# Expert choice of tiles 1 to 3 moved one unit sooner, and the order of the row gathers with it

## The reference

```python
q = (t @ wq).reshape(PEER_BLOCK, PEER_HEADS, 2, PEER_DQ // 2)
s = jnp.einsum('tpcd,pckd->tpck', q, sub_keys)
s1, i1 = lax.top_k(s[:, :, 0], PEER_TOPK)
s2, i2 = lax.top_k(s[:, :, 1], PEER_TOPK)
cand = s1[..., :, None] + s2[..., None, :]        # 16 x 16 sums
cidx = i1[..., :, None] * PEER_NKEYS + i2[..., None, :]
top, pos = lax.top_k(cand, PEER_TOPK)             # (flattened)
idx = jnp.take_along_axis(cidx, pos, axis=-1)
g = jax.nn.softmax(top, axis=-1)
a = jax.nn.gelu(jnp.einsum('tpkd,td->tpk', u[idx], t))
return jnp.einsum('tpk,tpkd->td', g * a, v[idx])
```

## Time and profile before

| | |
|---|---|
| median of 3 runs | 3128.29 us (3120.03 to 3139.96) |
| the profiled execution | 3147.13 us, span 3145.3 us |
| busy share of PE, DVE, ACT, POOL | 77%, 61%, 31%, 37% |
| gathers begin and end | 622.3 us, 2438 us |
| first memset of `half(0)` | 1559.13 us |
| mean granted clock of TensorE | 0.871 |

### The profile page before, as it was taken

The page is one execution under the profiler, slowest core; times in us unless marked ns, Lnnn a source line. Parts: engine busy times, 40 slices in busy tenths (PEclk is TensorE's granted clock), DMA queues, the critical chain, the costliest instruction groups (busy, mean ns, idle before and its releaser), DMA issues.

```text
span 3145.3 us, 43836 instructions
## 1 busy us (share of the span) xinstructions
PE 2415.9 (77%) x16608; PEld 1758.0 (56%) x16608; DVE 1930.2 (61%) x4058; ACT 976.8 (31%) x1694; POOL 1154.5 (37%) x1028
## 2 busy tenths in 40 slices
PE   7898996896044545565475898976999999999998
PEld 5666775545000000111174777742677889996998
DVE  3221866488945655476688877764344576666665
ACT  4443655311000000000032433422433455455544
POOL 0000000067755657577756565567455000000000
PEclk8998998998567887788786999976999999998999
DMA  6232111289978989899988999999899545552454
GB/s 270 98 111 83 48 42 53 95 315 352 330 289 316 369 320 360 314 350 348 360 307 304 330 408 408 408 375 336 300 406 397 180 137 179 186 192 68 146 184 147
DMA packets 218945, 803.92 MB, mean 256 GB/s; under 512 B 24432, under 2 KB 27760, under 8 KB 214768
## 3 DMA queue, kind: packets, MB, share of 16 engines
q0 software_dynamic: 147456, 536.94, 45.4%
q1 hardware_dynamic: 71280, 264.19, 23.7%
HBM read 798.93 MB, written 2.10 MB: 255 GB/s over the span
## 4 chain that ended last, share of the span: by engine, by line
PE 33%; DVE 19%; issue 11%; POOL 8%; DMA 7%; another core or an unknown queue 3%; ACT 1%; DVEq 0%; SPq 0%; POOLq 0%; ACTq 0%
PE ps L1817 9%; PE ps L1819 8%; PE ps L1818 8%; DVE pe_ring L2522 7%; PE ps L1757 4%; DMA pe_ring<-in_v,pe_vidx 3%; POOL pe_ring L1700 3%; POOL pe_ring L1706 3%; DVE la_w_lo L2570 3%; DMA pe_ring<-in_u,pe_idx 1%; PE ps L1896 1%; POOL pe_more L1700 1%; PE ps L1905 1%; PE ps L1922 1%
## 5 line engine op out<-in xcount | busy, mean ns | idle before, releaser
L1757 PE MATMUL ps<-pe_ring,pe_spot 128*32 128x512 f32 x1632 | 430.4, 754 | 245.6 <-DMA pe_ring<-in_v,pe_vidx 192.2
L1700 POOL DMA_INDIRECT pe_ring<-in_u,pe_idx x415 | 489.7, 1180 | 289.8 <-issue 178.6
L2522 DVE CUSTOM_DVE_ANT_0 pe_ring<-pe_ring,pe_htok 128x1024 f32<-128x1024 f32 x415 | 495.4, 1222 | 136.8 <-DMA pe_ring<-in_u,pe_idx 119.7
L1817 PE MATMUL ps<-la_h_hi,la_w_hi 128*128 128x256 f32 x1856 | 537.5, 290 | 32.8 <-DVE la_w_lo L2570 21.5
L1819 PE MATMUL ps<-la_h_hi,la_w_lo 128*128 128x256 f32 x1856 | 529.0, 285 | 2.6 <-issue 2.2
L1818 PE MATMUL ps<-la_h_lo,la_w_hi 128*128 128x256 f32 x1856 | 528.2, 285 | 1.8 <-issue 1.7
L1706 POOL DMA_INDIRECT pe_ring<-in_v,pe_vidx x408 | 438.4, 1074 | 236.3 <-issue 115.8
L2570 DVE TENSOR_TENSOR la_w_lo<-la_w_raw,la_w_hi 128x1024 fp32r<-128x1024 f32 (+1 forms) x368 | 440.1, 1196 | 69.3 <-ACT la_w_hi L2182 48.7
L2182 ACT ACTIVATE la_w_hi<-la_w_raw 128x1024 fp32r<-128x1024 f32 (+1 forms) x368 | 379.7, 1034 | 306.6 <-DMA la_w_raw<-in_down 77.8
L1817 PEld LDWEIGHTS ps<-la_h_hi,la_w_hi 128*128 128x128 f32 x1856 | 354.8, 191 | 70.7 <-DVE la_w_lo L2570 33.3
L1757 PEld LDWEIGHTS ps<-pe_ring,pe_spot 128*32 128x32 f32 x1632 | 85.2, 126 | 486.2 <-issue 313.1
(11 more groups left out here) (366 smaller groups left out, 3960.9 us busy)
## 6 DMA issues: line engine op xcount, KB each, us to landing
la_w_raw<-in_gate SPq DMA_DIRECT2D x88, 512.0 KB
la_w_raw<-in_up SPq DMA_DIRECT2D x88, 512.0 KB
la_w_raw<-in_down SPq DMA_DIRECT2D x64, 448.0 KB
la_w_raw<-in_a_in SPq DMA_DIRECT2D x40, 512.0 KB
wring<-in_w_in SPq DMA_DIRECT2D x32, 512.0 KB, 3.8
la_w_raw<-in_down SPq DMA_DIRECT2D x32, 512.0 KB
xT<-in_w_mod SPq DMA_DIRECT2D x8, 1024.0 KB, 4.8
hT<-in_w_mod SPq DMA_DIRECT2D x8, 1024.0 KB, 4.9
```

The source lines that it names most:

```text
L1700: pool.indirect_dma_start(row(n), None, io["u"], bass.IndirectOffsetOnAxis(idx[:, t, j:j + 1], 0)).then_inc(land[GATHERS[n][0]], 16)
L1757: return pe.matmul(ps[PER * grp:PER * grp + PER, half, :], spot[:, j // TOKENS % 2, grp, lo:lo + PER], row(n)[:, half * 512:(half + 1) * 5 ...
L1817: pe.matmul(slot(n), parts_hi[:, n % SPLIT, i, :], hi[:, k, :], start=first, stop=False)
L2522: dve.tensor_tensor_reduce(row(n), row(n), htok[:, t, :], 1.0, 0.0, ALU.mult, ALU.add, dots[:, t % 2, j:j + 1]).then_inc(dot_done, 1)
```

## The change

Three things are changed. In `gathers()` the v rows that stood behind the last unit of tile 1 and behind the last group of tile 2 are put ahead instead: 28 v rows of tile 0 go first in place of 16, and 12 of tile 1 in place of 2. On DVE each choose of tiles 1 to 3 is made one unit sooner (in the groups of tile 2, one group sooner): choose(1,0) and choose(1,1) stand together behind `weigh(0)`, choose(1,2), (1,3) and (2,0) behind dots 31, 63 and 95 of tile 1, choose(2,1) behind `weigh(1)`, and choose(2,2) to (3,3) behind groups 0 to 5 of tile 2; nothing is chosen behind group 6. On ACT the exps follow. `turn_indices(1)` now stands behind v row 96 instead of 108, and `token_indices(1)` behind dot 98 instead of 116.

```diff
-    TURN_AT, SUM_AT, SQUARES_AT = (108, 84), (16, 32), 60
+    TURN_AT, SUM_AT, SQUARES_AT = (96, 84), (16, 32), 60
...
-        v_next = P - 4 * (UNIT_U // 2 + 12)
+        v_next = P - 4 * UNIT_U // 2 - 3 * 12
...
-            if j % UNIT_U == UNIT_U - 1:
+            if j % UNIT_U == UNIT_U - 1 and j + 1 < P:
...
-        v_next = P - GROUPS_U * (GROUP_U + GROUP_V)
+        v_next = P - GROUPS_U * GROUP_U - (GROUPS_U - 1) * GROUP_V
...
-            if j % GROUP_U == GROUP_U - 1:
+            if j % GROUP_U == GROUP_U - 1 and j + 1 < EARLY:
...
             choose(1, 0)
+            choose(1, 1)
             for j in range(HK):
                 dot(1, j)
                 if j % UNIT_U == UNIT_U - 1 and j + 1 < HK:
-                    choose(1, (j + 1) // UNIT_U)
-                if j == 116:
+                    ahead = (j + 1) // UNIT_U + 1
+                    choose(1 + ahead // 4, ahead % 4)
+                if j == 98:
                     token_indices(1)
             weigh(1)
-            choose(2, 0)
+            choose(2, 1)
...
-                choose(2 + (group >= 3), (group + 1) % 4)
+                if group + 1 < GROUPS_U:
+                    choose(2 + (group >= 2), (group + 2) % 4)
```

More of the change, by code:

```diff
@@ L2407, in _ @@
             exps(1, 0)
+            exps(1, 1)
             place_weights(0, 2)
             place_weights(0, 3)
-            exps(1, 1)
+            exps(1, 2)
             place_weights(0, 4)
-            exps(1, 2)
             place_weights(0, 5)
+            exps(1, 3)
             place_weights(0, 6)
-            exps(1, 3)
+            exps(2, 0)
             place_weights(0, 7)
             gelu(1)
-            exps(2, 0)
             place_weights(1, 0)
@@ L2422, in _ @@
             exps(2, 1)
+            exps(2, 2)
             place_weights(1, 2)
-            exps(2, 2)
             place_weights(1, 3)
@@ L2427, in _ @@
             place_weights(1, 4)
+            exps(3, 0)
             square(0)
-            exps(3, 0)
             place_weights(1, 5)
+            exps(3, 1)
             place_weights(1, 6)
-            exps(3, 1)
+            exps(3, 2)
             place_weights(1, 7)
-            exps(3, 2)
             exps(3, 3)
```

## The result

| | before | after |
|---|---|---|
| median of 20 runs each | 3135.39 us (3119.84 to 3162.19) | 3107.03 us (3088.57 to 3124.26) |
| ratio | | 0.9903, 95% interval 0.9880 to 0.9927 |
| the profiled execution | 3147.13 us, span 3145.3 | 3104.64 us, span 3102.8 |
| first memset of `half(0)` | 1559.13 us | 1512.35 us |

The change gains 28 us by the medians (23 to 38 by the interval of the ratio), against 64 forecast: 3107 lies above the range of 3044 to 3098. The prediction's 3128.29 was the median of three runs; over 20 it is 3135.39. The half begins 46.8 us sooner, where 66 were forecast (1493).

A forecast was written before the change was run, and what follows sets the result against it. The prediction took no engine as full all the time, but the stream of gathers, broken by POOL's waits, as the bound. Terms of 14.9 + 30.4 + 15.05 + 4 = 64 us off 3128.3 gave 3064 us, range 3044 to 3098.

The forecast's parts named there:

- Term 1: Start of tile 1: twelve more v rows fill 14.9 us of POOL's 21.31 us wait before u row 0.
- Term 2: Inside tile 1: with chooses a unit sooner, POOL's waits before u rows 32, 64 and 96 go, 30.4 us.
- DVE stays the faster one and catches up: Inside tile 1, a unit of 60 gathers: the stream needs 77 us, DVE's 32 dots and one choose 54 to 71.
- Term 3: Start of tile 2: POOL's 15.05 us wait before u row 0 goes; ACT's two added waits cost 0.
- Term 4: Way into the first half of the last layers: choose(3,3) comes a group sooner; 3.5 to 8.5 us, taken as 4.
- Does the gain last: From gather 568 to the end: the order is the old one, and all 64 us are carried through.
- five waits: POOL's idle before u rows 0, 32, 64, 96 of tile 1 and 0 of tile 2, 66.73 us in sum.
- slower, by the idle without releaser: Rival: POOL's twelve waits without releaser, 870 to 1560 us, each grow to 10.38 us; 31 us slower, 3159; chance 0.05.
- The wait changes its name: Rival: in tile 2 POOL waits for buffers behind late dots; 35 us back, gain 29, 3099 us; chance 0.11.

The follow-up runs named there:

- old_again: The kernel before the change, unaltered, profiled on the same chip as `changed_again`; 3119.3 us in one run, that chip's median of the old kernel being 3125.7.
- changed_again: The changed kernel, unaltered, run again on a chip where the old kernel takes 3125.7 us; 3101.0 us, ratio 0.9908.
- early_chooses_t1: The old kernel with only the chooses inside tile 1 made a unit of dots sooner and ACT's exps to suit; 3097.2 us, ratio 0.9915.
- changed_third: The changed kernel, unaltered, on a chip where the old kernel takes 3038.9 us; 3002.8 us, ratio 0.9875.
- one_input_again: The changed kernel with dots of tile 1 and rows 0 to 55 of tile 2 as one-input sums, on the chip of `changed_third`; 2982.1 us, ratio 0.9814.

## Why the prediction was wrong

The sum of the prediction adds waits, and what POOL's gathers take was the same before and after in it. By the profiled pair, 42.5 us apart, against the terms (numbers of gathers as above):

- **Ahead of the change**: 5.5 us by gather 143, where the kernels are the same. So this much of the 42.5 isn't the change's. The profiled old execution lay 11.7 us over its median and the new one 2.4 under its own, which leads from 42.5 to the 28.4 of the medians.
- **Term 1**, start of tile 1, 14.9: measured 10.5 (gathers 143 to 156 in 29.85 us, before 40.35). The twelve rows did fill the wait, but stops drew choose(1,0) out to 41.3 us.
- **Term 2**, inside tile 1, 30.4: measured 9.1 (344.6 to 335.6). POOL's waits there went from 46.4 to 14.0 us, as forecast; the excess rose from 14.4 to 38.1. **This is the step that failed**: "DVE stays the faster one and catches up". It does catch up, at 1.15 us a dot, but while it does, a gather takes two dots, 2.29 us, where the sum took 1.28. The 23.7 us of added excess account for the 21.3 that the term fell short.
- **Term 3**, start of tile 2, 15.05: measured 15.1 (31.0 to 15.9), and gathers 396 to 568 take 254.5 us against 255.7, as assumed. ACT's added waits cost nothing seen.
- **Term 4**, way into the half, 4: measured 5.3 (gathers 568 to 596), the wait before 596 falling from 12.50 to 6.92.
- **Does the gain last**: of 46.7 us at gather 596, 42.5 are left at the end.

The second pair, `old_again` and `changed_again` on one chip, gives -1.6 for term 1 (there was little to win, the wait being 1.59 us), 6.4 for term 2 (waits 33 to 11 us, excess 31 to 46) and 10.4 for term 3. So term 2 is in both pairs the one that falls short most. The medians of `early_chooses_t1` don't bear the split out: term 2 alone is worth 26.6 us there, 17 to 36 by the interval. How the loss splits over the terms is thus read from single executions. That excess was added and that waits had been counted too long, all profiles show; what each costs in time on this sort of chip stays open.

The second fault is in the size of all waits: 66.73 us came from one execution on a chip with late updates. In `old_again` the same five waits are

```profile
876.07 0.94 POOL L1700 DMA_INDIRECT pe_ring<-in_u,pe_idx  x1 [1.59 <-issue]
...
969.37 0.94 POOL L1700 DMA_INDIRECT pe_ring<-in_u,pe_idx  x1 [9.99 <-issue]
...
1063.10 0.94 POOL L1700 DMA_INDIRECT pe_ring<-in_u,pe_idx  x1 [9.93 <-PE ps L1757]
...
1153.91 0.94 POOL L1700 DMA_INDIRECT pe_ring<-in_u,pe_idx  x1 [6.91 <-issue]
...
1249.84 0.94 POOL L1700 DMA_INDIRECT pe_ring<-in_u,pe_idx  x1 [8.54 <-issue]
```

These are 37 us, with chooses of 16.8, 20.6, 20.8, 22.7 and 20.9 us before them; only the first choose was in time, and 9 to 11 us were expected behind it, not 1.59. An estimate from 7.8 us to the last dot, a choose of 16.8 and 1.245 us a gather gives 39 us; as the waits here still hold some 4 us of late updates each, it may be high. The earlier trace rows held the warning, 7.74 us of idle in choose(1,0); that choose and the ones before three of the four other waits took 27.2 to 28.4 us. Those 10 us each were not the choose's work, so moving it could not win them; they turned up elsewhere (twelve chooses 291 us in all before, 304 after). 39 us less the 14 to 15.5 of added excess is 23.5 to 25, near the 24.7 and 28.4 that the medians give on chips with late updates; with the 39 an estimate, that may be luck.

Of the rivals, "slower, by the idle without releaser" named this idle and put its growth on POOL alone. Outside the five waits POOL's idle grew only from 33 to 41 us in the stretch, and DVE's chooses by 13. "The wait changes its name" (3099) came nearest in time, but not by its mechanism: POOL waits for no dot there, and for sums, that is for buffers of v rows, 11.0 us in place of 2.9. What replaced the waits has no name in a list of waits at all, since it stands in the *duration* of POOL's instructions. It could be read before, in the groups by line of the old kernel, here those of 857.9 to 1548.5 us (busy us, mean ns, idle before):

```profile
L1706 POOL DMA_INDIRECT pe_ring<-in_v,pe_vidx x181 | 188.4, 1041 | 76.1 <-issue 52.8 <-remote 18.4 <-PE ps L1757 5.0
```

It says 1041 ns on average, where I took 0.94 us.

The Trainium skill, "SBUF — State Buffer", section "SBUF: two separate sides", states the rule I didn't weigh: VectorE with two SBUF inputs and a GpSimd operation that reads SBUF exclude each other for the whole instruction, and the later one is fully blocked. The traces agree: beside back-to-back dots with two inputs an issue takes 1.99 us and ends 0.89 us after the next dot's start, beside one-input dots 0.94. The rule that I did weigh, in the Trainium skill, "Runtime: NRT & Kernel Launch", section "Instruction fetch mechanics", that crossing into a block is mostly hidden, would have given 70 us. The idle stayed, and loads of instructions don't explain it: in the stop from 865.0 to 873.9 us no packet of an instruction queue moves, in that from 876.2 to 885.1 one, and `changed_third`, which has no such stops, moves the same 133 packets.

## What to carry to other kernels

A wait that is removed lets the engine behind it run beside something else: ask not only who waits next, but which pair of engines now runs at the same time, and look at the mean duration of their instructions where they already do. A mean of a short instruction that is 10% longer than its usual time (1.04 us against 0.94) can be a stall in disguise. Where a wait's length has idle in it that has no releaser, take the work of the awaited step without it, and take the wait from two executions or more before it goes into a sum.

## What the hardware showed

- A gather's issue (0.94 us, one every 1.24) beside dots with two SBUF inputs back to back (one every 1.145) locks to two dots, 2.29 us. Beside dots with one input (1.22 us each) the issues keep their 0.94 us: excess of 440 gathers 4 to 7 us against 45 to 73. TENSOR_TENSOR with two inputs in SBUF does the same: 1.44 us at 512 numbers, and from 1500 to 2460 us of the changed kernel the 79 issues of which more than half ran beside `la_w_lo<-la_w_raw,la_w_hi` (1024 numbers) took 1.30 us on average, up to 1.99.
- The unbroken stream then runs at 408 GB/s and a DMA share of 1.03 (`one_input_again`); POOL's 1.245 us a gather and the DMA engines' 1.28 are nearly the same limit.
- Updates of semaphores came 3 to 9 us late on three chips and never on two, with the same kernels; the old kernel takes 3126 to 3135 us on the one sort and 3039 to 3046 on the other. With them POOL waits 29 to 128 us in the stretch, and taking out the long issues made it only 8 to 13 us shorter, against 37 without them. What makes them is open.
